# A conditioned two-block network on one core: how the first feed-forward stage computes the modulation

## The reference, cut to what matters

```python
c_act = silu(c)                                        # c: 1 x 1024
for l in range(2):
    mod = c_act @ ada_w[l] + ada_b[l]                  # 1024 -> 6 * 1024
    sh_m, sc_m, gt_m, sh_f, sc_f, gt_f = split(mod, 6)
    h = rms_norm(x, norm_mix[l]) * (1 + sc_m) + sh_m
    x = x + gt_m * mixer_l(h)                          # hybrid mixer, then retention
    h = rms_norm(x, norm_ffn[l]) * (1 + sc_f) + sh_f
    x = x + gt_f * swiglu(h, ffn_w_in[l], ffn_w_out[l])
return second_block(x)                                 # two more mixers and feed-forwards
```

## Time and profile before

| what | value |
|---|---|
| median of 3 runs | 2818.15 us (2817.92 to 2819.38) |
| profiled execution: span, first to last instruction | 2817.4 us |
| median of the runs less that span | 0.75 us |
| TensorE matmul busy | 2739.0 us, 97% |
| TensorE weight load busy | 2184.2 us, 78% |
| VectorE busy | 1416.0 us, 50% |
| ScalarE busy | 961.9 us, 34% |
| GpSimd busy | 548.8 us, 19% |
| mean granted TensorE clock | 0.995 |
| HBM read | 283.46 MB, 104 GB/s |

### The profile page before, as it was taken

How to read it: one execution, slowest core, us unless ns; L and a number is a source line. 1 busy time by engine, 2 the same in 40 slices (tenths; PEclk the granted TensorE clock), 3 DMA queues, 4 the chain that set the end, 5 groups by cost and what they waited for, 6 DMA issues and landing times.

```text
span 2817.4 us, 31915 instructions
## 1 busy us (share of the span) xinstructions
PE 2739.0 (97%) x13258; PEld 2184.2 (78%) x13258; DVE 1416.0 (50%) x2086; ACT 961.9 (34%) x1264; POOL 548.8 (19%) x422
## 2 busy tenths in 40 slices
PE   7999999999999999999999999999999999999998
PEld 4877777888887787788888867778888865788886
DVE  5655657575463333362323465655355465554453
ACT  3545544222243313342222343342223344322222
POOL 2252641100122212121001200022022100121121
PEclk9999999999999999999999999999999999999999
DMA  6223233465232232224522322222322311222322
GB/s 249 89 76 106 90 141 129 175 221 190 90 112 80 74 108 79 75 93 121 159 103 78 121 81 68 82 90 71 116 100 75 118 57 64 90 86 88 119 72 71
DMA packets 51088, 296.28 MB, mean 105 GB/s; under 512 B 6617, under 2 KB 6745, under 8 KB 25088
## 3 DMA queue, kind: packets, MB, share of 16 engines
q1 hardware_dynamic: 44912, 276.58, 27.8%
q0 software_dynamic: 4736, 15.34, 2.1%
q10 hardware_dynamic: 1296, 2.32, 0.2%
HBM read 283.46 MB, written 8.65 MB: 104 GB/s over the span
## 4 chain that ended last, share of the span: by engine, by line
PE 90%; DVE 5%; ACT 3%; issue 1%; POOL 1%; DMA 0%; ACTq 0%; DVEq 0%; POOLq 0%
PE ps L218 89%; PE ps L1336 1%; DVE hl L306 1%; ACT whi L200 1%; DVE wlo L211 1%; ACT F L1353 0%; DMA x<-in_x 0%; ACT hh L290 0%; DVE F L418 0%; DVE hl L422 0%; DVE ada L466 0%; DVE F L833 0%; ACT hh L436 0%; DVE x L681 0%; ACT E L1353 0%
## 5 line engine op out<-in xcount | busy, mean ns | idle before, releaser
L218 PE MATMUL ps<-hh,whi 128*128 128x512 f32 x2088 | 824.7, 395 | 8.5 <-DVE hl L306 4.5
L218 PE MATMUL ps<-hl,whi 128*128 128x512 f32 x2088 | 813.9, 390 | 0.0
L218 PE MATMUL ps<-hh,wlo 128*128 128x512 f32 x2088 | 813.2, 389 | 0.0
L211 DVE TENSOR_TENSOR wlo<-raw,whi 128x2048 fp32r<-128x2048 f32 (+2 forms) x235 | 497.5, 2117 | 508.4 <-ACT whi L200 506.3
L218 PE MATMUL ps<-R,whi 128*128 128x512 f32 x2080 | 659.2, 393 | 9.4 <-DVE wlo L211 2.8
L200 ACT ACTIVATE whi<-raw 128x2048 fp32r<-128x2048 f32 (+2 forms) x235 | 409.6, 1743 | 732.6 <-PE ps L218 732.4
L218 PEld LDWEIGHTS ps<-hh,whi 128*128 128x128 f32 x2088 | 392.4, 188 | 99.2 <-issue 8.1
L218 PEld LDWEIGHTS ps<-R,whi 128*128 128x128 f32 x2080 | 390.8, 188 | 98.2 <-issue 9.0
L218 PEld LDWEIGHTS ps<-hl,whi 128*128 128x128 f32 x2088 | 392.2, 188 | 83.0
L218 PEld LDWEIGHTS ps<-hh,wlo 128*128 128x128 f32 x2088 | 392.6, 188 | 81.3 <-issue 2.2
L218 PE MATMUL ps<-R,wlo 128*128 128x512 f32 x1040 | 405.1, 390 | 0.0
(11 more groups left out here) (345 smaller groups left out, 2479.6 us busy)
## 6 DMA issues: line engine op xcount, KB each, us to landing
F<-in_ada SPq DMA_DIRECT2D x32, 1024.0 KB, 4.8
raw<-in_fs0in SPq DMA_DIRECT2D x22, 1024.0 KB, 5.4
raw<-in_fs1in SPq DMA_DIRECT2D x22, 1024.0 KB, 4.7
raw<-in_fc0in SPq DMA_DIRECT2D x22, 1024.0 KB, 4.7
raw<-in_fc1in SPq DMA_DIRECT2D x22, 1024.0 KB, 4.7
Rf<-in_ada0h SPq DMA_DIRECT2D x24, 512.0 KB, 3.5
raw<-in_fs0out SPq DMA_DIRECT2D x16, 704.0 KB, 4.3
raw<-in_fs1out SPq DMA_DIRECT2D x16, 704.0 KB, 4.2
```

The source lines that it names most:

```text
L211: e.tensor_tensor(m.wlo[n % 2][:, 0:size], m.raw[m.slot[n]][:, 0:size], m.whi[n % 2][:, 0:size].bitcast(F32), SUB).then_inc(*s.up("wlo", n))
L218: return e.matmul(out, l, r, start=start, stop=stop, skip_group_check=True)
```

## The change

The 28 modulation slabs of the stage `s0` are stored transposed: output channels on partitions, the 1024 input channels along the row, two groups of 128 outputs side by side. silu(c) is wanted as a row on every partition: ScalarE issues a load of c, broadcast to 128 partitions, into `crow` (the two `tmp` buffers, now one tile) behind the row norms of the stage before, and takes its Silu at u = 1. On VectorE one multiply-and-sum over 1024 columns (`tensor_tensor_reduce`) gives 128 modulation values at once, straight into `mod`; two of them and one bias addition make a step. The partition sums on TensorE and their waits are gone. At u = 1 `dve_slab` now stands ahead of the modulation step. The loads of SP and GpSimd wait for the new signal `ada_dot`.

```diff
-        self.tmp = [sb(f"tmp{i}", T)[:, :] for i in range(2)]
+        self.crow = sb("tmp", 2 * T)
+        self.tmp = [self.crow[:, i * T:(i + 1) * T] for i in range(2)]
...
@@ pe_ffn
             n = m.at[name + "in", u]
-            pe_ffn_ada(e, s, m, st, n)
...
             slab = m.at[f"{name}out{half}", n]
-            pe_ffn_ada(e, s, m, st, slab)
...
@@ act_ffn
             if conv or u:
                 act_slab(e, s, m, n + 1)
+            if st == "s0" and u == 1:
+                s.wait_ge("crow_in")
+                e.activation(m.crow[:, :], m.crow[:, :], table(e, s, ACT.Silu)).then_inc(*s.up("crow"))
...
@@ dve_ffn
             if conv or u:
-                dve_ffn_ada(e, s, m, st, n)
+                if u > 1:
+                    dve_ffn_ada(e, s, m, st, n)
                 dve_slab(e, s, m, n + 1)
+                if u == 1:
+                    dve_ffn_ada(e, s, m, st, n)
...
@@ sp_ffn
-                        s.wait_ge("ada_k", "f", k - 3, 7)
-                    l, j = ADA_F[k]
-                    e.dma_start(m.f(2048 * (k % 3), 2048), m.dram[f"ada{l}"][j]).then_inc(*s.dma(f"ada_in{k % 3}", k))
+                        s.wait_ge("ada_dot", k - 3, 1)
+                    e.dma_start(m.f(2048 * (k % 3), 2048), m.dram["adat"][k]).then_inc(*s.dma(f"ada_in{k % 3}", k))
...
@@ dve_ffn_ada
-    if 0 < i <= len(ADA_F):
-        l, j = ADA_F[i - 1]
-        dve_ada_bias(e, s, m, 48 * l + 2 * j, 2, 7, "ada_sum", ("f", i - 1))
-    if i < len(ADA_F):
-        s.wait_ge(f"ada_in{i % 3}", i)
-        if i >= 2:
-            s.wait_ge("ada_sum", "f", i - 2)
-        run(dve_ada(e, s, m, m.f(2048 * (i % 3), 2048), i % 2, ("f", i)))
-
-
-def pe_ffn_ada(e, s, m, st, n):
-    i = n - m.at["fs0in", 0] - 2
-    if st == "s0" and 0 <= i < len(ADA_F):
-        if i:
-            s.wait_ge("mod", "f", i - 1)
-        pe_ada(e, s, m, i % 2, 2, 7, ("f", i))
+    l, j = ADA_F[i]
+    at = 48 * l + 2 * j
+    s.wait_ge("crow")
+    s.wait_ge(f"ada_in{i % 3}", i)
+    for c in range(2):
+        w = m.f(2048 * (i % 3) + 1024 * c, 1024)
+        e.tensor_tensor_reduce(out=w, in0=w, in1=m.crow[:, :], scale=1.0, scalar=0.0, op0=MUL, op1=ADD,
+                               accum_out=m.mod[:, at + c:at + c + 1]).then_inc(*s.up("ada_dot", i, c))
+    s.wait_ge("ada_dot", i, 1)
+    e.tensor_tensor(m.mod[:, at:at + 2], m.mod[:, at:at + 2], m.col("adab", at, 2), ADD).then_inc(*s.up("mod", "f", i))
...
@@ act_between
     act_rs(e, s, m, st, 3)
+    if st == "hyb":
+        e.dma_start(m.crow[:, :], m.dram["crow"].to_broadcast([P, 1024])).then_inc(*s.dma("crow_in"))
     act_norm(e, s, m, st, first)
...
@@ pool_ret
-    s.wait_ge("ada_k", "f", 27, 7)
+    s.wait_ge("ada_dot", 27, 1)
```

More of the change, by code:

```diff
@@ L879, in sp_ffn @@
                     if k >= 3:
-                        s.wait_ge("ada_k", "f", k - 3, 7)
-                    l, j = ADA_F[k]
-                    e.dma_start(m.f(2048 * (k % 3), 2048), m.dram[f"ada{l}"][j]).then_inc(*s.dma(f"ada_in{k % 3}", k))
+                        s.wait_ge("ada_dot", k - 3, 1)
+                    e.dma_start(m.f(2048 * (k % 3), 2048), m.dram["adat"][k]).then_inc(*s.dma(f"ada_in{k % 3}", k))
 def dve_ffn_ada(e, s, m, st, n):
     i = n - m.at["fs0in", 0] - 1
-    if st != "s0" or i < 0:
+    if st != "s0" or not 0 <= i < len(ADA_F):
         return
-    if 0 < i <= len(ADA_F):
-        l, j = ADA_F[i - 1]
-        dve_ada_bias(e, s, m, 48 * l + 2 * j, 2, 7, "ada_sum", ("f", i - 1))
-    if i < len(ADA_F):
-        s.wait_ge(f"ada_in{i % 3}", i)
-        if i >= 2:
-            s.wait_ge("ada_sum", "f", i - 2)
-        run(dve_ada(e, s, m, m.f(2048 * (i % 3), 2048), i % 2, ("f", i)))
-def pe_ffn_ada(e, s, m, st, n):
-    i = n - m.at["fs0in", 0] - 2
-    if st == "s0" and 0 <= i < len(ADA_F):
-        if i:
-            s.wait_ge("mod", "f", i - 1)
-        pe_ada(e, s, m, i % 2, 2, 7, ("f", i))
+    l, j = ADA_F[i]
[8 more added lines that the diff above has]
+    e.tensor_tensor(m.mod[:, at:at + 2], m.mod[:, at:at + 2], m.col("adab", at, 2), ADD).then_inc(*s.up("mod", "f", i))
 def pe_toeplitz(e, s, m):
@@ L3599, in layout @@
     o["x"] = a["x"][0].T.reshape(8, P, T)
-    for l in range(2):
-        o[f"ada{l}"] = slabs(a["ada_w"][l], run(6144, 256), 256)
+    o["ada0"] = slabs(a["ada_w"][0], run(2048, 256), 256)
+    w = a["ada_w"].transpose(0, 2, 1).reshape(2, 24, 2, P, 1024).transpose(0, 1, 3, 2, 4)
+    o["adat"] = np.stack([w[l, j].reshape(P, 2048) for l, j in ADA_F])
+    o["crow"] = a["c"].reshape(1, 1024)
     o["ada0h"] = slabs(a["ada_w"][0][:, 2048:5120], run(3072, 128), 128)
```

## The result

The changed kernel took 2803.27 us (median of 4 runs, 2802.37 to 2804.95), the kernel before beside it 2818.62 us (4 runs, 2817.92 to 2819.38). The ratio is 0.9944, with a 95% interval of 0.9930 to 0.9958: 15.4 us less, and no change lies well outside the interval. The profiled execution took 2802.62 us, its span 2800.8 us. TensorE is still 91% of the chain of waits.

What follows compares the result with a forecast made beforehand. TensorE was taken as the bound, with 90% of the chain of waits. Removed matmuls (13.5 us) and the closed wait at the third slab (4.1) gave 17.6 us off 2818.15: 2800.5 us, with 3 us allowed below and 2804 as upper end.

Steps and rivals of the forecast that it cites:

- The pairs: Two one-column modulation matmuls at each weight-slab seam on TensorE leave; 27 at 0.50 us save 13.5 us.
- The third slab: First feed-forward stage: TensorE's wait for wlo goes, 6.14 us against 2.04 for its 9 steps, saving 4.1 us.
- Their sum: Matmuls removed at the seams plus the closed wait for wlo: 17.6 us less in all.
- The check against the second feed-forward stage: Second stage without its two bias matmuls takes 355.15 us, 17.54 below the first, against 17.6 from the two terms.
- The multiply-and-sum: New VectorE operation over 1024 columns, priced from L1298 at 1.23 us, plus 0.083 us to read the sum out.
- Half rate: Rival, 11%: VectorE needs two cycles a column, a step takes 5.0 us, the fourth slab waits for wlo: 2803.5 us.
- The bound of 5.2 us for a step: In the 33-matmul slabs a VectorE modulation step may grow from 3.97 to 5.2 us before TensorE waits.
- The gap stays: Rival, 4%: ScalarE delays the high half, wlo is late again at the third slab, up to 4.1 us: 2804.6 us.
- the pair's price belongs to the boundary: Rival, 2%: the half microsecond comes from the slab boundary, not the one-column matmuls; only the wlo gap goes: 2814 us.
- VectorE as the bound: Rival, 3%: sums in the first feed-forward stage's slabs too slow to hide; at quarter rate 60 us, 2861 us.
- the 0.75 us that the sum adds: Difference between the kernel before's run median, 2818.15 us, and its profiled span, 2817.4 us, left unchanged in the forecast.

Runs made afterwards that it cites:

- the pair put back: Changed kernel with two one-column fp32 matmuls, result unused, added on TensorE at each of the 28 seams: median 2816.91 us, ratio to before 0.9991.
- the two kernels with the other order: Changed kernel with first sums ahead of wlo: 2806.32 us, ratio 0.9959; kernel before with wlo ahead of the first step: 2820.11 us, ratio 1.0009.
- the double sums: Changed kernel with each multiply-and-sum done twice, the second into an unused column: median 2809.92 us, ratio 0.9969.
- four times the sums: Changed kernel with each multiply-and-sum done four times: 2909.30 us, ratio 1.0325.

## Why the prediction was right

*The pairs: 27 x 0.50 = 13.5 us.* Right; the pair put back cost 0.50 us in each steady slab and 14.4 us over the 28.

*The third slab: 4.1 us.* Right, gap and low clock both gone. The pair put back leaves 3.4 us of it, and the two kernels with the other order show that it took both edits: wlo first gains nothing while the sums are on TensorE.

*Their sum: 17.6 us.* The stage fell by 17.61. The check against the second feed-forward stage, 355.15 us, was met within 0.1.

*The multiply-and-sum: 1.23 us.* Measured 1.22 where nothing met it. With GpSimd's subtraction beside it the delay was 1.1 us (I had allowed 1.3), in 18 of the 56, and 18 of GpSimd's subtractions in the stage took 1.54 us instead of 1.29. The Trainium skill ("SBUF — State Buffer", section "Who interferes with whom") says that a VectorE instruction with two SBUF inputs contends with a GpSimd instruction that reads SBUF; this trace agrees, with 2.32 against 1.22 us.

*Half rate* is out, near as its 2803.5 us lies to the median: TensorE waits nowhere in the stage, and 1024 columns with both operands in SBUF and a sum took 1.22 us, what L1298 with one in PSUM gives for that length. The Trainium skill ("Vector Engine (DVE) Microarchitecture Reference", section "Points that are easy to get wrong") has the scalar-tensor-tensor shape at half throughput with two non-bf16 SBUF sources; this trace has 1.22 us where half rate would take 2.3, so for this operation the measurement decides, and no trace tells whether the chip runs it as that shape. The rival's price was too low, though: the double sums, a stand-in for it, cost 5.8 us in the stage and not up to 3, mostly by the two changes of slab kind.

*The bound of 5.2 us for a step* held within 0.3 us: 5.0 left 0.17 us in one short slab and cost 0.3 in three others. *The gap stays* and *the pair's price belongs to the boundary* did not occur. *VectorE as the bound* did not occur either; four times the sums showed the mechanism within the price worked out.

*What was off.* The median came out 2.8 us above the forecast of 2800.5. It is inside the range because the upper end had been drawn out to 2804 for the half-rate rival, which did not occur; the 1.4 us by which the runs spread would not have reached it. So that the range held is luck in part, while the 17.6 us of the stage are not. Three small things make up the 2.8 us. The profiled execution of the kernel before, 2819.38 us, was 1.2 above its median, so the 0.75 us that the sum adds are not what lies between a run's time and its span: no run shows that, and every one has 1.75 to 2.0 us, in both kernels. The profiled execution of the changed kernel was 0.65 us below its median. The rest, about 0.9 us, is that the profiled executions lie 16.8 us apart and not 17.6: the extra low-clock stretch in the tail cost 1.5 us, and about 0.5 came back before the stage and in it. The prediction took what lies outside the stage as unchanged on the strength of one trace, and allowed for such a stretch only downwards ("I allow 3 us below"). Whether the change brings the stretch on, or it only fell so in these executions, stays open.

## What to carry to other kernels

Where TensorE is the bound, count what interrupts its stream by the price at the seam and not by its work: a one-column fp32 matmul costs as much here as a full 128x512 one of the rounded type, 0.22 us, and one of two columns in the rounded type half of that. A sum over the contraction that VectorE can do along the row costs nothing while its step fits into the slab, so work out the largest step that fits first. And when an edit moves work out of one engine, look again at the order on the others: here the new order belongs to the 4.1 us of the third slab, and alone it gained nothing (a stage 2.0 us longer). A difference of 1 to 3 us between two traces can be low-clock stretches in code that nobody edited, so compare the edited stage by itself.

## What the runs showed of the hardware that I had not expected

A wait of TensorE is not followed by a low clock each time: the wait of 1.7 us for wlo in the kernel before was, the wait of 2.8 us at the fourth slab with double sums was not (clock 1.00 from 473 to 480 us), and one of 1.6 us ahead of the stage was in one trace of the changed kernel and not in the other. In the tail, where the stretches fell repeated between the two traces of each program: 2035.67 and 2035.64, 2037.17 and 2037.09, 2034.00 and 2034.04 us, with each stretch worth about 1.5 us. So two traces of one kernel can agree to 0.1 us over these 2 ms and still differ by 2 us ahead of them.
